# Products of ones beside three norms and in the scan, 64x64 pieces on all four quadrants, and PSUM banks picked by age, in a two-block float32 kernel

## The reference, cut to what matters

```python
y = x32 * lax.rsqrt(jnp.mean(x32 * x32, axis=-1, keepdims=True) + NORM_EPS)     # tags m0, r, m1
...
kk = heads(k * k_k)
kk = kk / jnp.maximum(jnp.sqrt(jnp.sum(kk * kk, axis=-1, keepdims=True)), 1e-12) # inner norm 1: sums, spread
...
sa = jnp.einsum('bhvk,bhk->bhv', state, a_t)                                     # 512 steps, 16 heads of 64
state = (state * w_t[:, :, None, :] + sa[..., None] * b_t[:, :, None, :]
         + v_t[..., None] * k_t[:, :, None, :])
y_t = jnp.einsum('bhvk,bhk->bhv', state, r_t)
...
y = (y - mean) * lax.rsqrt(var + GN_EPS)                                         # inner norm 2: gsum, gn
out = ((y + bonus).reshape(bsz, seq, d).astype(h.dtype) * g) @ w_o
```

## Time and profile before

| | us |
|---|---|
| median of 3 runs (lowest, highest) | 2473.8 (2471.53, 2474.29) |
| the profiled execution | 2468.86 |
| its span in the trace | 2467.1 |
| PE busy, DVE busy, ACT busy in it | 2411.2, 1625.7, 1081.5 |
| mean granted clock | 0.994 |

### The profile page before, as it was taken

The page is one execution under the profiler, slowest core; times in us unless marked ns, Lnnn a source line. Parts: engine busy times, 40 slices in busy tenths (PEclk is TensorE's granted clock), DMA queues, the critical chain, the costliest instruction groups (busy, mean ns, idle before and its releaser), DMA issues.

```text
span 2467.1 us, 43151 instructions
## 1 busy us (share of the span) xinstructions
PE 2411.2 (98%) x18172; PEld 2053.6 (83%) x18172; DVE 1625.7 (66%) x2640; ACT 1081.5 (44%) x1696; POOL 223.1 (9%) x226
## 2 busy tenths in 40 slices
PE   8999999999999999999999999999999999999998
PEld 7787989886678887898989889898678987889888
DVE  7867979667856556675768667575355744557558
ACT  4224454327653334545456333343255544334334
POOL 0100000110220000000000010111221000011010
PEclk9999999999999999999999999999999999999999
DMA  8664565662310003364644345355112431336335
GB/s 318 194 195 136 162 208 183 193 216 69 98 40 4 5 30 128 92 165 120 161 112 135 106 117 165 94 140 159 61 52 69 142 98 48 99 111 159 123 95 142
DMA packets 101057, 304.62 MB, mean 123 GB/s; under 512 B 11280, under 2 KB 13584, under 8 KB 100352
## 3 DMA queue, kind: packets, MB, share of 16 engines
q1 hardware_dynamic: 80944, 237.38, 29.5%
q0 software_dynamic: 19920, 64.48, 10.8%
HBM read 297.62 MB, written 4.19 MB: 122 GB/s over the span
## 4 chain that ended last, share of the span: by engine, by line
PE 84%; DVE 9%; ACT 3%; issue 2%; SPq 1%; DMA 1%; DVEq 0%; ACTq 0%
PE ps L784 19%; PE ps L790 16%; PE ps L788 16%; PE ps L837 5%; PE ps L840 5%; PE ps L842 5%; PE ps L800 3%; PE ps L803 3%; DVE WLs L2127 2%; PE ps L849 1%; ACT WHs L1417 1%; PE ps L999 1%; SPq L3165 1%; PE ps L1012 1%; DMA raw<-in_cw_in_k 1%
## 5 line engine op out<-in xcount | busy, mean ns | idle before, releaser
L2127 DVE TENSOR_TENSOR WLs<-raw,WHs 128x1024 fp32r<-128x1024 f32 (+3 forms) x497 | 507.8, 1022 | 258.7 <-ACT WHs L1417 254.8
L784 PE MATMUL ps<-HH,WHs 128*128 128x512 f32 x1728 | 654.4, 399 | 6.2 <-ACT HH L1512 2.6
L1417 ACT ACTIVATE WHs<-raw 128x1024 fp32r<-128x1024 f32 (+3 forms) x516 | 455.6, 884 | 310.4 <-PE ps L842 140.9
L790 PE MATMUL ps<-HH,WLs 128*128 128x512 f32 x1462 | 570.4, 390 | 2.7 <-DVE WLs L2127 2.7
L788 PE MATMUL ps<-HL,WHs 128*128 128x512 f32 x1462 | 569.4, 389 | 0.0
L784 PEld LDWEIGHTS ps<-HH,WHs 128*128 128x128 f32 x1728 | 323.5, 188 | 79.1 <-issue 12.4
L837 PE MATMUL ps<-HT,WHs 128*128 128x256 f32 x1344 | 375.5, 279 | 5.9 <-DVE X L2214 5.8
L842 PE MATMUL ps<-HT,WLs 128*128 128x256 f32 x1344 | 373.3, 278 | 0.3 <-DVE WLs L2127 0.2
L840 PE MATMUL ps<-HT,WHs 128*128 128x256 f32 x1344 | 373.0, 278 | 0.0
L790 PEld LDWEIGHTS ps<-HH,WLs 128*128 128x128 f32 x1462 | 274.4, 188 | 62.2 <-DVE WLs L2127 4.6
L788 PEld LDWEIGHTS ps<-HL,WHs 128*128 128x128 f32 x1462 | 274.8, 188 | 56.0 <-issue 2.2
(11 more groups left out here) (475 smaller groups left out, 3625.0 us busy)
## 6 DMA issues: line engine op xcount, KB each, us to landing
ada<-in_adaw POOLq DMA_DIRECT2D x80, 512.0 KB, 4.6
raw<-in_f1gu_b SPq DMA_DIRECT2D x20, 512.0 KB, 3.5
raw<-in_f2gu_b SPq DMA_DIRECT2D x20, 512.0 KB, 3.5
raw<-in_f1gu_a_m SPq DMA_DIRECT2D x18, 512.0 KB, 3.5
raw<-in_w_in_m SPq DMA_DIRECT2D x18, 512.0 KB, 3.5
raw<-in_f2gu_a_m SPq DMA_DIRECT2D x18, 512.0 KB, 3.5
ada<-in_adaw SPq DMA_DIRECT2D x16, 512.0 KB, 16.4
raw<-in_cw_in_m SPq DMA_DIRECT2D x16, 512.0 KB, 3.6
```

The costliest lines, as they stand in the source:

```text
L784: pe.matmul(o[m], WHs[:, s, w], hi, start=k == 0, stop=False)
L790: t = pe.matmul(o[m], WLs[:, s, w], hi, start=False, stop=k == DEPTH_K[name] - 1)
L1417: act.activation(WHs[:, SLOT[v], 0:n], piece(v), ACT.Copy).then_inc(*S.up("w_hi", ("hi", v)))
L2127: dve.tensor_tensor(WLs[:, s, 0:n], piece(v), WHs[:, s, 0:n].bitcast(F32), SUB).then_inc(*S.up("w_lo", ("lo", v)))
```

## The change

1. `keep(idle, n)` issues n products of `ones` by `ones` (128x128 weights, 128 columns) into a bank that nothing reads before it is overwritten. The three norms m0, r and m1 take a bank "idle" and issue 3 before the wait for the last square, 3 before the wait for the reciprocal, and 3, 14 or 3 after both spreads. In the scan 3 stand ahead of ls of chunk 4, 2 ahead of each u of chunks 4 to 7, and 2 ahead of the first gate block.
2. w, ls and u put both halves `hf` into one group, two banks side by side, in an order that uses all four quadrants. They wait for the second half's input before the first product, where each half waited for its own. For that the second half's matrix is stored with the partition halves swapped: pa of `hf` 1 becomes twice as many products of 64 columns, px only changes places.
3. The sums and the spread of both inner norms become 64x64 pieces, in two banks by half: 64x64 weights on one column, and 64x64 weights on 64 columns.
4. In the scan alone banks are picked by age: each user has an entry in `STAYS` (how long it works, how long its bank is then taken, in units of the plan), and `take` picks the bank whose plan frees it first.
5. State and y of chunk 6 stand behind `gate_weights` 0, and `gate_weights` 1 ahead of ls of chunk 7, ahead of the first gate block. The order of TensorE's own work stays.

```diff
+STAYS = {"p": (3, 5), "q": (3, 6), "tt": (2, 5), "ls": (1, 5), "ys": (3, 6), "u": (1, 5), "state": (2, 6), "yu": (3, 4), "pa": (6, 9),
+         "pk": (6, 9), "px": (3, 6), "at": (3, 8), "kt": (3, 8), "gsum": (3, 5), "gn": (3, 14), "bonus": (3, 8), "w": (2, 6),
+         "vt": (5, 6), "gw2": (3, 4)}
...
         b = self.turn
+        if self.by_age:
+            b = min((i for i in range(8) if i not in self.held), key=lambda i: (self.until[i], (i - self.turn) % 8))
+            self.stay(key, b)
         self.turn = (b + 1) % 8
...
-gate_in ls6 sums2 root2 u6 state6 y6
+gate_in ls6 sums2 root2 u6
...
-    out += [("gate_weights", 0), ("through", 3, 1, "ls"), ("gate_weights", 1), ("gate", 0), ("through", 3, 1, "u"), ("gate", 1),
+    out += [("gate_weights", 0), ("through", 3, 0, "state"), ("through", 3, 0, "y"), ("gate_weights", 1), ("through", 3, 1, "ls"), ("gate", 0),
+            ("through", 3, 1, "u"), ("gate", 1),
...
+            def keep(idle, n):
+                for _ in range(n):
+                    pe.matmul(idle[:, 0:128], ones[:, :], ones[:, :], start=True, stop=True)
...
-            def norm(tag):
-                total(tag)
+            def norm(tag, after):
+                idle = bank("idle")
+                total(tag, acc, idle)
+                keep(idle, 3)
                 spread(tag)
-                if tag in TWICE:
-                    spread(tag, 0, "rb2")
+                spread(tag, 0, "rb2")
+                keep(idle, after)
+                B.forget("idle")
...
-                        o = bank("unit", f)
+                        o = bank_two("unit", f)
                         on.wait_ge(*S.at("ur", f // 4))
                         for c in range(4):
-                            for p in range(2):
-                                n = 8 * f + 2 * c + p
-                                t = pe.matmul(o[half(p), 128 * c:128 * c + 128], ur[:, n:n + 1].to_broadcast([128, 64]), ident[:, :],
-                                              start=True, stop=True)
+                            for u in range(2):
+                                for p in range(2):
+                                    n = 32 * (f // 4) + 16 * p + 4 * (f % 4) + c
+                                    t = pe.matmul(o[half(p), u, 64 * c:64 * c + 64], ur[half(u), n:n + 1].to_broadcast([64, 64]),
+                                                  ident[half(u), half(u)], start=True, stop=True)
...
                 if part == "u":
-                    for hf in range(2):
-                        o = bank("u", cc, hf)
-                        on.wait_ge(*S.at("T", c, hf, 4))
-                        on.wait_ge(*(S.at("wk", cc, hf) if cc else S.at("w", c, hf)))
-                        for f, i, p in heads(hf):
-                            h, n = home(p, u), 128 * f + 64 * u
-                            t = pe.matmul(o[h, 64 * i:64 * i + 64], T[h, n:n + 64], Wk[h, 512 * u + 64 * f:512 * u + 64 * f + 64],
-                                          start=True, stop=True)
-                        t.then_inc(*S.up("mm_scan", ("full", "u", cc, hf)))
+                    o = [bank("u", cc, hf) for hf in range(2)]
+                    if cc > 3:
+                        keep(o[0], 2)
+                    on.wait_ge(*S.at("T", c, 1, 4))
+                    on.wait_ge(*(S.at("wk", cc, 1) if cc else S.at("w", c, 1)))
+                    for i in range(4):
+                        for hf in range(2):
+                            for p in range(2):
+                                f, j = 4 * hf + i, u ^ hf
+                                h, n = home(p, j), 128 * f + 64 * j
+                                t = pe.matmul(o[hf][home(p, u), 64 * i:64 * i + 64], T[h, n:n + 64], Wk[h, 512 * u + 64 * f:512 * u + 64 * f + 64],
+                                              start=True, stop=True)
+                    t.then_inc(*S.up("mm_scan", ("full", "u", cc, 0), ("full", "u", cc, 1)))
...
                 if m == 0:
+                    keep(o, 2)
```

More of the change, by code:

```diff
@@ L286, in take, with stay @@
         return b, earlier
+    def stay(self, key, *banks):
+        works, stays = STAYS[key[0]]
+        self.now += works
+        for b in banks:
+            self.until[b] = self.now + stays
     def take_two(self, key, hold=False):
@@ L292, in take_two @@
         b = self.turn
+        if self.by_age:
+            b = min((i for i in range(0, 8, 2) if i not in self.held and i + 1 not in self.held),
+                    key=lambda i: (max(self.until[i:i + 2]), (i - self.turn) % 8))
+            self.stay(key, b, b + 1)
         self.turn = (b + 2) % 8
@@ L307, in release @@
             self.held.discard(self.place[key] + i)
+            self.until[self.place[key] + i] = self.now + 5
 MLP = ["abc", "abc"]
@@ L920, in keys @@
                     if what == "sums":
-                        o = bank("sums", f)
+                        o = bank_two("sums", f)
                         for j in range(4):
@@ L957, in group @@
                 tokens = lambda u: slice(128 * c + 64 * u, 128 * c + 64 * u + 64)
-                if part in ("pa", "pk"):
+                if part == "pa" and hf:
+                    o = bank_two(part, c, hf)
+                    for i, f in enumerate(fs):
+                        ready(c, f)
+                        for x, r in ((L, 0), (R, 1)):
+                            for u in range(2):
+                                for p in range(2):
+                                    j, n = u if r else 1 - u, 128 * i + 64 * r
+                                    t = pe.matmul(o[home(p, j), j, n:n + 64], A[half(p), f, tokens(u)], x[half(p), f, tokens(u)], start=True, stop=True)
+                    t.then_inc(*S.up("mm_scan", ("full", part, c, hf)))
+                elif part in ("pa", "pk"):
                     o, x = bank_two(part, c, hf), A if part == "pa" else K
@@ L1040, in through @@
                 if part == "ls" and cc:
[L1041 to L1047 removed]
+                    o = [bank("ls", cc, hf) for hf in range(2)]
+                    if cc == 4:
+                        keep(o[0], 3)
+                    on.wait_ge(*S.at("S", cc - 1, 1))
+                    for i in range(4):
+                        for hf in range(2):
+                            for p in range(2):
+                                f = 4 * hf + i
+                                t = pe.matmul(o[hf][home(p, u ^ hf), 64 * i:64 * i + 64], L[half(p), f, cs], ST[half(p), 64 * f:64 * f + 64],
+                                              start=True, stop=True)
+                    t.then_inc(*S.up("mm_scan", ("full", "ls", cc, 0), ("full", "ls", cc, 1)))
                     o = bank("ys", cc)
@@ L1097, in group_norm @@
                 if part == "sums":
-                    o = bank("gsum", c)
+                    o = bank_two("gsum", c)
                     on.wait_ge(*S.at("gsq", c))
                     for f in range(8):
-                        t = pe.matmul(o[:, 2 * f:2 * f + 2], gsq[:, f], bones[:, 0:128:64], start=True, stop=True)
+                        for u in range(2):
+                            for p in range(2):
+                                t = pe.matmul(o[half(u), p, f:f + 1], gsq[half(p), f, 64 * u:64 * u + 64], bones[half(p), 64 * p:64 * p + 1],
+                                              start=True, stop=True)
                     t.then_inc(*S.up("mm_scan", ("full", "gsum", c)))
```

75 lines of the change are left out of this document (45 added, 30 removed).

## The result

| | before | after |
|---|---|---|
| median of the timed runs, us | 2473.94 (10 runs, 2470.37 to 2477.1) | 2480.85 (10 runs, 2477.1 to 2487.93) |
| profiled execution, its span | 2468.86, 2467.1 | 2485.55, 2483.8 |
| MATMUL rows of the program | 18172 | 19042 |

The ratio is 1.0031 (95% interval 1.002 to 1.0041): slower by 6.9 us, where 20.6 us less were forecast. The traces show what happens and where; how much it is worth is taken from the medians.

What follows compares the result with a forecast made beforehand. The prediction took TensorE, with 84% of the span, as the bound, so products taken from its queue count unless another engine's answer ends later. Its terms summed to -20.6 us, from 2473.8 to 2453.2 for the median; range 2442 to 2467.

Steps and rivals of the forecast that it cites:

- norms: Norms r and m1: products of ones keep the clock up, so each norm gains 0.9 us, m0 nothing: -1.8 us.
- inner norm of the keys: Keys' norm ahead of the scan: 64x64 pieces shorten spreads and sums, less low clock behind them: -5.8 us, bounds -7 and -2.
- w, u, ls, pa: Scan: both halves on four quadrants shorten w, u and ls by 10.4 us; pa's added rows cost 0.4.
- group norm: Scan: 64x64 pieces make the group norm's sums and spreads quicker: -6.3 us, bounds -7.5 and -3.
- banks by age and order: Scan and first gate block: a bank wait at ls of chunk 4 goes, -1.1 us; gate weights come earlier, -2.7.
- products of ones in the scan: Scan: the added products of ones and their switches cost TensorE time: +4.3 us, bounds +1 and +5.
- answers that come late: Scan: with TensorE's part shorter, each chunk's fixed chain and instruction fetches show: +2.8 us, bounds 0 and +10.
- Rival (e): Scan: TensorE stands in the same waits and the clock falls; with half of 54 stretches low, 2496 us; chance 0.05.
- rival (b): u, key spreads and group spreads: products on the same rows don't overlap, so gains halve: +5.4, 2459 us; chance 0.06.
- rival (c): m1, r and the gate: products of ones don't hold the clock, low stretches stay: 2458 us; chance 0.05.
- Rival (a): Scan: waits for other engines' answers take half of the 20 us that products give: 2463 us; chance 0.25.

Runs made afterwards that it cites:

- experiment 9: The changed kernel without the products of ones in its scan: 2478.4 us, ratio to before 1.0016 (1.0003 to 1.003).
- experiment 3: The kernel before with only w, u, ls, pa and the group norm in their new pieces, old banks and order, no products of ones: 2483.3 us, ratio 1.0033.
- experiment 5: A separate kernel of products and loads only, no waits: 2048 rows of 64x64 on four quadrants took 28.1 ns a row with stops, 16.4 while running.
- experiment 1: The kernel before with only the products of ones beside the norms m0, r and m1: 2473.2 us against 2475.59, ratio 0.9995 (0.9985 to 1.0006).
- experiments 4 and 10: The kernel before with only banks by age and the last chunk's new order: 2471.36 us, ratio 0.998; the kernel before with that order alone: ratio 0.9987.

## Why the prediction was wrong, step by step

| step | forecast, us | measured alone, by ratio x 2474 |
|---|---|---|
| norms | -1.8 | -1.2 (-3.7 to +1.5) |
| inner norm of the keys | -5.8 | +2.7 (-0.5 to +5.7) |
| w, u, ls, pa | -10.0 | +2.0 (-2.2 to +6.2) |
| group norm | -6.3 | +4.0 (0 to +8.2) |
| banks by age and order | -3.8 | -4.9 (-7.2 to -2.5) |
| products of ones in the scan | +4.3 | +3.7 (-0.5 to +7.9), after less experiment 9 |
| answers that come late | +2.8 | in the rows above |

The three pieces of the scan taken together are +8.2 (experiment 3). With -1.2, +2.7, -4.9 and +3.7 the parts add up to +8.5 us, against +7.7 (4.9 to 10.1) for the whole change by its ratio; their intervals are wide enough for that.

*The step that failed* is "answers that come late: +2.8". It saw the fetches (47, one per 4.5 us, and a stop of 1.0 with nothing to wait for) and took them for a small surcharge. They are a second limit beside the engine. 5970 rows by 28.1 ns, the stream's rate, are 168 us of before's 198.7. Of these rows 2816 (p, q and px: L999, L1012, L973) were quick ones in before already, and 2688 took 28 to 30 ns, which is just that limit and puts nothing by. Before lived on the 466 wide rows between them. The change took the engine's time for w, u, ls and the sums to half, added 474 rows, and bought stops: rows by 28.1 ns are now 181 us. In experiment 3, 6418 rows by 28.1 ns are 180 us and TensorE is busy 178: the supply has become the longer of the two. The waits called issue grew by 13.0 us there and by 12.9 in after; the step's term was 2.8 for these and late answers together. The step's upper bound, +10, was not enough either; from the forecast for the scan's pieces (-16.3 with w, u, ls, pa and the group norm) to what experiment 3 shows are 24.5 us.

The clock is a second term, and the sum had none for it in the scan. The runs give each execution's mean granted clock. Experiment 3's ten have 0.9866 on average, and before's 31 beside them 0.9904. The difference, 0.0038 of 2480 us, is 9.4 us at most (low clock costs nothing while TensorE stands), against 8.2 us by which that kernel is slower. Among its ten runs the one with the highest clock, 0.992, took 2475.75 us, as long as before's median of 2475.59; the one with the lowest, 0.982, took 2490.69. So in the scan's pieces the stops took back what the quick rows gave, and about what lies above before goes with the clock. After's ten have 0.9891 against 0.9906 for before's 83 runs beside the experiments, at most 4 of its 6.9 us. This is an estimate, not a test.

*Rival (e)*, slower because the clock falls, had a chance of 0.05 and named the sign. A lower clock there is. That it falls because TensorE stands more often isn't shown. The stream of experiment 5 stood 24.1 of 57.6 us at a clock of 1.00, and the traced scans of after and experiment 3 have the same 17 us of stops at 0.92 and 0.98. Nor did TensorE stand in "the same waits" but in new ones, those of the supply. Of the 15 us by which after's traced scan is longer, 11.2 are idle time (22.6 against 11.4) and 3.8 busy time, in which the gain of the pieces, some 9.6, is used up by lower clock and by the 26 rows of ones. What takes the clock down stays open. The prediction's reading that each fall "followed waits and products of one column" holds for r and m1; the fall at 927.2 came behind waits of 1.0, 0.4 and 1.5 us with products of 64 and 512 columns between.

*The inner norm of the keys.* The price was right and the stated bound was wrong: "banks in pairs while wr holds four can add waits" was given as an end at -2, which allows 3.8 us for them; the distance from the forecast to what was measured is 8.5 (5.3 to 11.5). The bound should have been worked out from the reader of the bank before: VectorE's HP product ended at 699.0 in before too (698.36 + 0.68), 3.5 us behind the next spread's start (695.6).

*Right*: some 14.5 to 16 ns a row for the pieces. This speaks against rival (b) and the rule that stood with it (the Trainium skill, "TensorE: Matmul & The Clock Gate", Part 3): the new u, with neighbours on the same rows of the array, takes 0.52 for 32 rows (846.31 to 846.83), 16 ns each. Also right: the clock after r and m1, and 2.9 us for m1 against 3.8; so rival (c) falls in the norms. That r and m1 together give 1.8 of the whole is inside the interval of experiment 1 and no more. The traces of experiments 4 and 10 bear out the bank and the gate's wait; in time, the two together are clear of noise, and the order alone is not. Rival (a) has a small share in experiment 3 (waits for other engines +3.0 us) and none in after, where they shrank.

The same for r, as forecast: from the spread to the dense product now 558.53 - 553.44 = 5.1 us, where it was 6.0, with the ones in between:

```profile
553.44 2.02 PE L788 MATMUL ps<-ident,r 128*128 128x128 f32 x16
555.30 3.29 PE L766 MATMUL ps<-ones 128*128 128x128 f32 x28
558.53 1.17 PE L818 MATMUL ps<-M0H,WHs 128*128 128x512 f32 x4
```

## What to carry to other kernels

Count TensorE's rows in a stage of small products and multiply by 28 ns. If that is as long as the engine would be busy after the change (here 180 and 178 us), a form that does the same work quicker with as many rows or more gains little, and TensorE stands for 1 to 3 us at the ends of blocks of 128 rows. A gain that is forecast by the engine's work alone is an upper bound. Spend quick pieces in bursts of at most 128 rows between wide products, and away from heavy loads; prefer fewer rows to quicker ones (this follows from the rate; no kernel with fewer rows was run). Before a group takes two banks at once, look up when the slowest reader of the pair ends, not only how long the products run.

## What had not been expected of the hardware

- TensorE's instructions came at one block of 128 rows (256 instructions) per 3.73 us in a stream of nothing else, and one per 6.2 to 6.5 us while 16 loads of 512 KB ran.
- A burst of 64x64 rows ran at most 255 rows before it stopped; bursts of 128, with 4 wide rows between, never did.
- A turn between 64x64 pieces and 128x128 products cost some 0.1 to 0.2 us (an estimate from two mixes) even in a stream without waits.
- Stops of 1.2 to 1.9 us after every 128 rows, 24.1 of 57.6 us, left the granted clock at 1.00; in the scan, with 17 us of stops, it was 0.98 in one trace and 0.92 in another.
- With products of ones beside them the norms r and m1 ran at a clock of 1.00, where it was 0.61 and 0.55. In the scan no such effect shows (0.92 with them, 0.95 without, one trace each).
